# HGRN layer of a fused two-block kernel: order of the score products by width, order of VectorE's products, waits of the output product

## The chip, the cores and the metric

The kernel runs on one core of one Trainium2 chip. The metric is the device time of one execution in microseconds. Before the change the median of three executions is 1775.12 us (1773.36 to 1782.58). All data are f32.

## The reference, cut to what matters

Two transformer blocks are computed for one sequence of 512 tokens of width 1024. The first has chunked attention, a short convolution and a mixture of 32 experts. The second has two layers: an even one (mLSTM and sparse attention) and an odd one, HGRN2. The change touches the odd layer only:

```python
def hgrn2_layer(h, w_in, b_in, lb, head_norm, w_out):
    proj = h @ w_in + b_in
    fp, iv, qp, z = jnp.split(proj, 4, axis=-1)
    logf = jnp.log(lb + (1.0 - lb) * jax.nn.sigmoid(fp))
    k = (1.0 - lb) * jax.nn.sigmoid(-fp)
    q = jax.nn.silu(qp)
    o = hgrn2_chunkwise(heads(q), heads(k), heads(iv), heads(logf))
    o = rms_norm_2(o.transpose(0, 2, 1, 3), head_norm)
    return (o * jax.nn.silu(z)) @ w_out

def step(Sst, xs):                     # one chunk of one head
    bcum = jnp.cumsum(gj, axis=-2)
    dec = exp(bcum[j] - bcum[s])       # s <= j, else 0
    A = einsum('jc,sc,jsc->js', qj, kj, dec)
    o = A @ vj + (qj * exp(bcum)) @ Sst
    S_new = exp(bL)[:, None] * Sst + (kj * exp(bL - bcum)).T @ vj
```

There are 8 heads of 128 channels. The kernel takes chunks of 128 tokens, which gives the same result: four chunks a for 512 tokens.

## The kernel before, in words

**The layer's stages.** The heads go in four pairs p = 0 to 3, each with two heads c = 0, 1. For a pair TensorE computes in the order of `group(p, n)`: n = 0, 1 the forget projection of the two heads, n = 2, 3 the query projection (`feat`, 16 MATMULs of 512 columns each, two for each of 8 f32 products), then the values and the gate z. For p = 0 the latter are plain products (`tok`); for p = 1 to 3 they are one product in Winograd's form with seven sub-products (`seventh`, n = 4 to 10 of `group`, each 16 MATMULs of 256 columns). The seven share three PSUM banks a, b, c in the order a, b, a, b, c, b, c, so VectorE takes a bank after each sub-product (`seventh` of the vector program, its n = 0 to 6), and the fourth sub-product, b again, waits until the second has been taken. "Second take" is that one; "round" is one pass of p = 1 to 3.

**The scores.** A head's 128 x 128 matrix A of a chunk is cut at every 32 tokens, since exp(bcum[j] - bcum[s]) can't be factored over long distances. For query block J (32 tokens, J = 0 to 3) there is one diagonal product of keys `Km` and queries `Qm` (32 weight columns, 32 moving columns, output partitions 32J to 32J + 31) and, for J > 0, one product of all earlier keys, `KJ` (32 J weight columns: 32, 64 or 96), with queries `Qs` (output partitions 0 to 32J - 1). `step(p, "scores", c)` does first three transposes of D (the state's keys), which wait for the semaphore "pr", and then these 28 products for the four chunks a, all into one bank. `step(p, "states", c)` and `step(p, "outs", c)` are the state updates and the outputs. `PLAN` (lines 111, 112) writes down where in a round each step comes: states, outs and scores of the round before at n = 0, 1, 2, 3, 5, the scores of the pair's own first head at n = 9; `PLAN_LAST` does so for the last pair, between the parts of the output product. A step of scores thus comes eight times.

**Operands of the scores.** `prep(p, c, part)` in the vector program makes them: part 0 the cumulated logs, part 1 six differences (`Qs`, `Qm`, three blocks of `KJ`, D); ScalarE's `powers` then raises them, in the order Qs, Km, Qm, KJ, D, b and eL, each with an increment of "eE"; part 2 multiplies the powers by q or k (Qs, Qm, Km, three blocks of KJ of 128, 256 and 384 elements) and part 3 multiplies D by k and b by q, and tells "pr". `queries(p, c)` multiplies the query projection by its sigmoid. VectorE runs its program strictly in the written order: in a round `seventh` n = 0, part 2 of `prep`, `seventh` n = 1, `seventh` n = 2, part 3 and so on.

**The output product.** After the last round TensorE transposes the normed outputs y (`turn_y`; ("yT", 0, i) the heads 0 to 3 of token tile i, ("yT", 1, 0) and ("yT", 1, 2) the heads 4, 5 of two tiles each), VectorE and ScalarE copy them to `yT`, and `part(i, h, ks)` multiplies tile i by half h of the output weight. Before the first part TensorE waits for all six copies (`evacuated`).

**Lines.** L411 is every product of TensorE, L414 every transpose; L1168 is every two-operand operation of VectorE, L1179 its three-operand form, L1195 its copies, L2296 every operation of ScalarE.

Of the kernel before, what the change touches and what calls it, by code (L numbers as in the profile page):

```python
# [163 lines left out]
def build(nc, T, out):  # L164
    with ExitStack() as ctx:
# [228 lines left out]
        def tensor(pe):  # L394
# [11 lines left out]
            def evacuated(*names):  # L406
                for n in names:
                    pe.wait_ge(F[n].free, F[n].at)
# [628 lines left out]
            def stage_e():  # L1037
                def group(p, n):
                    if n < 4:
                        used[f"o_x{p}"] = feat(("fx", p, n), weight(f"o_x{p}"), n * 128)  # L1040
                    elif p:
                        for s in range(2):
                            seventh(f"o_y{p}", 2 * n - 8 + s)
                    else:
                        turned("E", n - 4)
                        used["o_y0"] = tok(("ty", n - 4), weight("o_y0"), n - 4)
                        if n in (4, 6):
                            turn("E", n // 2)

                def step(p, what, c):  # L1050
                    q, vz = pQ[p % 2][:, c, :], pvz[p % 2]
                    if what == "scores":
                        f = fill(("bt", p, c))
                        pe.wait_ge(S("pr"), saw("pr"))
                        for a in range(3):
                            ins = tr(f.ap[:, a * 128:a * 128 + 128], D[:, a * 128:a * 128 + 128])
                        ins.then_inc(f.full, 1)
                        f = fill(("ba", p, c))
                        for a in range(4):
                            for J in range(4):  # L1060
                                cj = a * 128 + 32 * J
                                if J:
                                    oo, wd, _ = KJP[J - 1]
                                    mm(f.ap[0:wd, cj:cj + 32], KJ[:, oo + a * wd:oo + a * wd + wd], Qs[:, cj:cj + 32])
                                ins = mm(f.ap[32 * J:32 * J + 32, cj:cj + 32], Km[:, cj:cj + 32], Qm[:, cj:cj + 32])
                        ins.then_inc(f.full, 1)
                    elif what == "states":
                        f = fill(("bu", p, c))
                        evacuated(("bt", p, c), *([(f"o_y{p}", "a"), (f"o_y{p}", "b")] if p else [("ty", 3)]))
                        for a in range(3):  # L1070
                            ins = mm(f.ap[:, a * 128:a * 128 + 128], KlT[:, a * 128:a * 128 + 128],
                                     vz[:, a, c * 128:c * 128 + 128])
                        ins.then_inc(f.full, 1)
                    elif what == "outs":
                        f = fill(("bo", p, c))
                        evacuated(("ba", p, c), ("bu", p, c))
                        for a in range(4):
                            o_ = f.ap[:, a * 128:a * 128 + 128]
                            ins = mm(o_, at[:, a * 128:a * 128 + 128], vz[:, a, c * 128:c * 128 + 128], True, a == 0)
                            if a:  # L1080
                                ins = mm(o_, q[:, a * 128:a * 128 + 128], St[:, a * 128 - 128:a * 128], False, True)
                        ins.then_inc(f.full, 1)

                def turn_y(name, i, ks):
                    f = fill(name)
                    for j, k in enumerate(ks):
                        ins = tr(f.ap[:, j * 128:j * 128 + 128], y4[:, i, k * 128:k * 128 + 128])
                    ins.then_inc(f.full, 1)

                def part(i, h, ks):  # L1090
                    f = fill(("oo", ks[0], i, h))
                    for k in ks:
                        ins = mm(f.ap, yT[:, k, i * 128:i * 128 + 128], ws[h][:, k * 512:k * 512 + 512], k == ks[0], k == ks[-1])
                    ins.then_inc(f.full, 1)
                for n in (4, 5, 6, 7, 0, 1, 2, 3):
                    group(0, n)
                step(0, "scores", 0)
                for p in range(1, 4):
                    for n in range(11):
                        if (p, n) == (1, 5):  # L1100
                            pe.wait_ge(S("suma"), 7)
                        group(p, n)
                        if n in PLAN:
                            what, back, c = PLAN[n]
                            step(p - back, what, c)
                        if (p, n) == (3, 9):
                            pe.wait_ge(S("yk"), 3)
                            for i in range(4):
                                turn_y(("yT", 0, i), i, range(4))
                for i in (0, 2):  # L1110
                    f = fill(("yT", 1, i))
                    for j in range(4):
                        k = 4 + j % 2
                        ins = tr(f.ap[:, j * 128:j * 128 + 128], y4[:, i + j // 2, k * 128:k * 128 + 128])
                    ins.then_inc(f.full, 1)
                ws = [weight(f"o_o{h}") for h in range(2)]
                for i in range(4):
                    evacuated(("yT", 0, i))
                for i in (0, 2):
                    evacuated(("yT", 1, i))  # L1120
                for n in range(8):
                    part(n // 2, n % 2, range(6))
                    if n in PLAN_LAST:
                        step(3, *PLAN_LAST[n])
                pe.wait_ge(S("yk"), 4)
                for i in range(4):
                    turn_y(("yT", 2, i), i, range(6, 8))
                for i in range(4):
                    evacuated(("yT", 2, i))
                    for h in range(2):  # L1130
                        part(i, h, range(6, 8))
# [8 lines left out]
        def vector(v):  # L1140
# [940 lines left out]
            def stage_e():  # L2081
# [19 lines left out]
                def prep(p, c, part):  # L2101
# [19 lines left out]
                    elif part == 1:  # L2121
                        if heads_[0]:
                            full("ba", *heads_[0])
                        heads_[0] = (p, c)
                        tt(j16(Qs), b16, bc16(bs), SUB)
                        tt(j16(Qm), b16, bc16(bm), SUB, "k1")
                        for J, (_, wd, dst) in zip((1, 2, 3), KJP):
                            tt(dst, bs4[:, :, J:J + 1].to_broadcast([128, 4, wd]), b4[:, :, 0:wd], SUB, "k2" if J == 3 else "v")
                        tt(bb.rearrange("p (a n) -> p a n", a=4), eL.unsqueeze(2).to_broadcast([128, 4, 128]), b4, SUB, "k3")
                    elif part == 2:  # L2130
                        heard("eE")
                        tt(Qs, Qs, q, MUL)
                        heard("eE", 2)
                        tt(Qm, Qm, q, MUL)
                        tt(Km, Km, kk, MUL)
                        heard("eE")
                        k4 = kk.rearrange("p (a n) -> p a n", a=4)
                        for _, wd, dst in KJP:
                            tt(dst, dst, k4[:, :, 0:wd], MUL)
                    else:  # L2140
                        heard("eE")
                        tt(bb, bb, kk, MUL)
                        heard("eE", 2)
                        tt(q, b, q, MUL, "pr")

                def scores(p, c):
                    f = full("ba", p, c)
# [53 lines left out]
                z_gain(0)  # L2201
                prep(0, 0, 0)
                prep(0, 0, 1)
                queries(0, 0)
                prep(0, 0, 2)
                prep(0, 0, 3)
                queries(0, 1)
                scores(0, 0)
                prep(0, 1, 0)
                for p in range(1, 4):  # L2210
                    y, r = f"o_y{p}", row("b_ivz" + "+" * p)
                    prep(p - 1, 1, 1)
                    states(p - 1, 0)
                    prep(p - 1, 1, 2)
                    prep(p - 1, 1, 3)
                    sums_of_weight(y)
                    queries(p, 0)
                    scores(p - 1, 1)
# [3 lines left out]
                    states(p - 1, 1)  # L2222
                    for n in range(7):
                        seventh(y, n, behind(pvz[p % 2]), by_row(r))
                        if n == 0:
                            prep(p, 0, 2)
                        elif n == 2:
                            row_done(r)
                            prep(p, 0, 3)
                        elif n == 3:  # L2230
                            pair_squares(p - 1)
                        elif n == 4:
# [14 lines left out]
                    h_add(i, h, full("oo", k0, i, h))  # L2247
                prep(3, 1, 1)
                states(3, 0)
                prep(3, 1, 2)  # L2250
                prep(3, 1, 3)
                for n in range(3):
                    part(n // 2, n % 2, 0)
                scores(3, 1)
# [846 lines left out]
```

## Time and profile before

| | |
|---|---|
| runs | 1773.36, 1775.12, 1782.58 us |
| profiled execution | 1776.3 us, span 1774.5 us |
| mean granted TensorE clock | 0.985 |
| TensorE (PE) busy | 1711.0 us, 96% |
| weight loads (PEld) busy | 1000.1 us, 56% |
| VectorE (DVE) busy | 864.8 us, 49% |
| ScalarE (ACT) busy | 372.5 us, 21% |
| GpSimd (POOL) busy | 209.7 us, 12% |
| DMA | 308.61 MB, queue q1 40.1% and q0 2.9% of 16 engines |

The profile is of one execution; its own time is 1776.3 us, and the span from the first to the last instruction 1774.5. Times in rows are microseconds from the span's start. Busy times of PE are modelled ends of pipelined matmuls: two rows that follow without a gap overlap by part of the last MATMUL. The granted clock is a share of 2.4 GHz and has two levels in this trace, 1.0 and 0.5. The HGRN layer runs from about 1450 us to the end.

### The profile page before, as it was taken

Reading aid. Unit: us, or ns where it says so; the run is one execution under the profiler, and the core shown is the slowest. Engines: PE = TensorE matmul, PEld = TensorE weight load, DVE = VectorE, ACT = ScalarE, POOL = GpSimd, SP = SyncE. Lnnn points to the kernel's source line nnn. Section 1 sums busy time; section 2 is a strip of 40 time slices with the busy share of each in tenths; the row PEclk is TensorE's granted clock in tenths of the full one; section 3 lists DMA queues with packets and bytes.
Section 4 is the critical chain, followed back from the end, with each engine's and each line's share of the span. In section 5 each row is a group of like instructions: output and inputs, shape, how many; then the busy total and the mean of one; then the engine's idle time right before and its main releaser. Section 6 shows DMA issues by size and latency. Waiting matters only on the chain.

```text
span 1774.5 us, 19612 instructions
## 1 busy us (share of the span) xinstructions
PE 1711.0 (96%) x7538; PEld 1000.1 (56%) x7538; DVE 864.8 (49%) x1505; ACT 372.5 (21%) x659; POOL 209.7 (12%) x280
## 2 busy tenths in 40 slices
PE   7999999998899999999999999999799999999999
PEld 3878877675433333333434464768655544767664
DVE  3756743445332323232325348666755555557653
ACT  1122220001100000100003113320244325344430
POOL 1234310001000000000001100011145300000000
PEclk9999999998999999999999999999999999999999
DMA  7322121255699999999991214032300021112101
GB/s 279 113 88 91 48 107 53 95 221 206 270 403 426 427 425 428 426 427 424 427 397 60 71 48 125 42 120 101 128 22 1 13 92 63 48 48 95 48 1 48
DMA packets 27873, 308.61 MB, mean 174 GB/s; under 512 B 4415, under 2 KB 4703, under 8 KB 10368
## 3 DMA queue, kind: packets, MB, share of 16 engines
q1 hardware_dynamic: 21312, 289.21, 40.1%
q0 software_dynamic: 6464, 18.10, 2.9%
q8 instruction: 62, 1.02, 0.2%
q14 instruction: 35, 0.29, 0.0%
HBM read 306.57 MB, written 4.19 MB: 175 GB/s over the span
## 4 chain that ended last, share of the span: by engine, by line
PE 88%; DVE 7%; ACT 1%; DMA 1%; issue 1%; POOL 0%; DVEq 0%; SPq 0%; ACTq 0%
PE ps L411 84%; PE ps L414 5%; DVE arena L1168 4%; ACT arena L2296 1%; DVE arena L1179 1%; DMA arena<-in_rows 1%; DVE wring L1168 0%; DVE arena L1195 0%; DMA wring<-in_dense 0%; DVE small L1183 0%; DVE arena L1264 0%; POOL small L2708 0%; ACT L2296 0%; DVE HT L1195 0%; DVE H L1168 0%
## 5 line engine op out<-in xcount | busy, mean ns | idle before, releaser
L411 PE MATMUL ps<-arena 128*64 128x512 f32 (+13 forms) x2384 | 532.9, 400 | 10.5 <-DVE arena L1173 3.8
L411 PE MATMUL ps<-wring,arena 128*64 128x512 f32 (+2 forms) x1136 | 397.7, 580 | 5.0 <-DVE H L1168 2.5
L411 PEld LDWEIGHTS ps<-arena 128*64 128x64 f32 (+3 forms) x2384 | 244.0, 154 | 232.9 <-issue 216.9
L411 PE MATMUL ps<-wring,HT 128*128 128x512 f32 (+1 forms) x1040 | 362.9, 502 | 5.1 <-ACT HT L2296 1.9
L1168 DVE TENSOR_TENSOR arena<-ps,arena 128x512 f32<-128x512 f32 (+1 forms) x197 | 134.9, 685 | 466.1 <-PE ps L411 307.1
L411 PEld LDWEIGHTS ps<-wring,HT 128*128 128x128 f32 x1040 | 194.3, 191 | 143.6 <-issue 127.6
L2296 ACT ACTIVATE arena<-ps 128x512 f32<-128x512 f32 (+3 forms) x163 | 88.4, 543 | 629.9 <-PE ps L414 325.5
L411 PEld LDWEIGHTS ps<-wring,arena 128*64 128x64 f32 (+1 forms) x1136 | 148.5, 155 | 125.6 <-issue 122.1
L411 PE MATMUL ps<-HT,wring 128*128 128x512 f32 (+2 forms) x528 | 196.1, 537 | 0.5 <-DVE arena L1195 0.5
L411 PE MATMUL ps<-wring 128*128 128x256 f32 x816 | 189.3, 387 | 5.1 <-DVE arena L1168 5.1
L1168 DVE TENSOR_TENSOR H<-ps,H 128x512 f32<-128x512 f32 x182 | 125.9, 692 | 103.5 <-PE ps L411 93.1
L411 PEld LDWEIGHTS ps<-wring 128*128 128x128 f32 x816 | 155.7, 194 | 30.3 <-DVE arena L1168 7.1
L2296 ACT ACTIVATE arena<-arena 128x512 f32<-128x512 f32 (+10 forms) x123 | 85.2, 692 | 355.3 <-DVE arena L1168 335.5
L411 PEld LDWEIGHTS ps<-HT,wring 128*128 128x128 f32 (+1 forms) x528 | 98.1, 191 | 88.2 <-issue 82.5
L1168 DVE TENSOR_TENSOR arena<-arena 128x512 f32<-128x512 f32 (+12 forms) x203 | 123.3, 607 | 19.6 <-ACT arena L2296 7.2
L414 PEld LDWEIGHTS ps<-con,arena 128*128 128x128 f32 (+4 forms) x762 | 92.9, 159 | 62.7 <-issue 50.6
L414 PE MATMUL ps<-con,arena 128*128 128x128 f32 (+4 forms) x762 | 107.9, 283 | 19.6 <-DVE arena L1179 10.8
L1195 DVE COPY arena<-ps 128x512 f32<-128x512 f32 (+7 forms) x126 | 70.3, 558 | 91.6 <-PE ps L411 66.2
L411 PE MATMUL ps<-HT,arena 128*64 128x512 f32 (+1 forms) x272 | 106.0, 542 | 4.1 <-issue 3.4
L2296 ACT ACTIVATE arena<-arena,small 128x128 f32<-128x128 f32 (+3 forms) x124 | 66.5, 536 | 124.2 <-DVE small L1264 113.6
L411 PEld LDWEIGHTS ps<-HT,arena 128*64 128x64 f32 (+1 forms) x272 | 41.4, 155 | 61.0 <-issue 57.7
L1264 DVE CUSTOM_DVE_ANT_0 arena<-ps,arena 128x512 f32<-128x512 f32 (+3 forms) x96 | 47.2, 492 | 45.0 <-PE ps L411 34.7
(106 smaller groups left out, 951.9 us busy)
## 6 DMA issues: line engine op xcount, KB each, us to landing
wring<-in_w SPq DMA_DIRECT2D x48, 2048.0 KB, 20.2
wring<-in_dense SPq DMA_DIRECT2D x39, 2048.0 KB, 8.1
arena<-in_w SPq DMA_DIRECT2D x36, 2048.0 KB, 17.8
HT<-in_w SPq DMA_DIRECT2D x12, 2048.0 KB, 16.8
arena<-in_rows POOLq DMA_DIRECT2D x33, 256.0 KB, 5.1
H<-in_x SPq DMA_DIRECT2D x4, 512.0 KB, 4.2
arena<-in_relb POOLq DMA_DIRECT2D x8, 256.0 KB, 8.2
n_scratch<-arena POOLq DMA_DIRECT2D x4, 512.0 KB, 3.2
```

Of the source, the lines that this page charges most:

```text
L411: return nc.tensor.matmul(o, l, r, start=start, stop=stop, skip_group_check=True)
L414: return nc.tensor.transpose(o, i, ident[0:i.shape[0], 0:i.shape[0]])
L1168: done(nc.vector.tensor_tensor(o, a, b, op), tell)
L1179: done(nc.vector.scalar_tensor_tensor(o, a, s, b, op0, op1), tell)
L1195: done(nc.vector.tensor_copy(o, i), tell)
L1264: done(nc.vector.tensor_tensor_reduce(o, a, b, -1.0, 3.0e38, ADD, MIN, low), tell)
L2296: ins = nc.scalar.activation(o, i, fn, **k)
```

## The change

It has three parts. In `step(p, "scores", c)` all 16 diagonal products come first and then the others by J, so that weights of 32, 64 and 96 columns follow each other in three groups. The output product waits only for the copies of its own tile. VectorE's parts 2 and 3 of `prep` are cut into queries, keys, blocks, state and out; in a round, queries and keys come after `seventh` n = 0, the three products of the blocks after n = 1, state and out after n = 2, and the first wait is for three exponentials at once. For the very first head, keys, blocks and state come before `queries(0, 0)`. The number of operations of each engine and the DMAs are unchanged.

```diff
--- before.py
+++ after.py
@@ -1059,10 +1059,11 @@
                         for a in range(4):
                             for J in range(4):
                                 cj = a * 128 + 32 * J
-                                if J:
-                                    oo, wd, _ = KJP[J - 1]
-                                    mm(f.ap[0:wd, cj:cj + 32], KJ[:, oo + a * wd:oo + a * wd + wd], Qs[:, cj:cj + 32])
-                                ins = mm(f.ap[32 * J:32 * J + 32, cj:cj + 32], Km[:, cj:cj + 32], Qm[:, cj:cj + 32])
+                                mm(f.ap[32 * J:32 * J + 32, cj:cj + 32], Km[:, cj:cj + 32], Qm[:, cj:cj + 32])
+                        for J, (oo, wd, _) in zip((1, 2, 3), KJP):
+                            for a in range(4):
+                                cj = a * 128 + 32 * J
+                                ins = mm(f.ap[0:wd, cj:cj + 32], KJ[:, oo + a * wd:oo + a * wd + wd], Qs[:, cj:cj + 32])
                         ins.then_inc(f.full, 1)
                     elif what == "states":
                         f = fill(("bu", p, c))
@@ -1114,11 +1115,9 @@
                         ins = tr(f.ap[:, j * 128:j * 128 + 128], y4[:, i + j // 2, k * 128:k * 128 + 128])
                     ins.then_inc(f.full, 1)
                 ws = [weight(f"o_o{h}") for h in range(2)]
-                for i in range(4):
-                    evacuated(("yT", 0, i))
-                for i in (0, 2):
-                    evacuated(("yT", 1, i))
                 for n in range(8):
+                    if n % 2 == 0:
+                        evacuated(("yT", 0, n // 2), ("yT", 1, n // 4 * 2))
                     part(n // 2, n % 2, range(6))
                     if n in PLAN_LAST:
                         step(3, *PLAN_LAST[n])
@@ -2127,21 +2126,34 @@
                         for J, (_, wd, dst) in zip((1, 2, 3), KJP):
                             tt(dst, bs4[:, :, J:J + 1].to_broadcast([128, 4, wd]), b4[:, :, 0:wd], SUB, "k2" if J == 3 else "v")
                         tt(bb.rearrange("p (a n) -> p a n", a=4), eL.unsqueeze(2).to_broadcast([128, 4, 128]), b4, SUB, "k3")
-                    elif part == 2:
-                        heard("eE")
+                    elif part == "queries":
                         tt(Qs, Qs, q, MUL)
-                        heard("eE", 2)
                         tt(Qm, Qm, q, MUL)
+                    elif part == "keys":
                         tt(Km, Km, kk, MUL)
+                    elif part == "blocks":
                         heard("eE")
                         k4 = kk.rearrange("p (a n) -> p a n", a=4)
                         for _, wd, dst in KJP:
                             tt(dst, dst, k4[:, :, 0:wd], MUL)
-                    else:
+                    elif part == "state":
                         heard("eE")
                         tt(bb, bb, kk, MUL)
+                    else:
                         heard("eE", 2)
                         tt(q, b, q, MUL, "pr")
+
+                def weighed(p, c, part):
+
+                    if part == 0:
+                        heard("eE", 3)
+                        prep(p, c, "queries")
+                        prep(p, c, "keys")
+                    elif part == 1:
+                        prep(p, c, "blocks")
+                    else:
+                        prep(p, c, "state")
+                        prep(p, c, "out")
 
                 def scores(p, c):
                     f = full("ba", p, c)
@@ -2201,9 +2213,12 @@
                 z_gain(0)
                 prep(0, 0, 0)
                 prep(0, 0, 1)
+                heard("eE", 3)
+                for x in ("keys", "blocks", "state"):
+                    prep(0, 0, x)
                 queries(0, 0)
-                prep(0, 0, 2)
-                prep(0, 0, 3)
+                prep(0, 0, "queries")
+                prep(0, 0, "out")
                 queries(0, 1)
                 scores(0, 0)
                 prep(0, 1, 0)
@@ -2211,8 +2226,8 @@
                     y, r = f"o_y{p}", row("b_ivz" + "+" * p)
                     prep(p - 1, 1, 1)
                     states(p - 1, 0)
-                    prep(p - 1, 1, 2)
-                    prep(p - 1, 1, 3)
+                    for x in range(3):
+                        weighed(p - 1, 1, x)
                     sums_of_weight(y)
                     queries(p, 0)
                     scores(p - 1, 1)
@@ -2222,11 +2237,10 @@
                     states(p - 1, 1)
                     for n in range(7):
                         seventh(y, n, behind(pvz[p % 2]), by_row(r))
-                        if n == 0:
-                            prep(p, 0, 2)
-                        elif n == 2:
+                        if n < 3:
+                            weighed(p, 0, n)
+                        if n == 2:
                             row_done(r)
-                            prep(p, 0, 3)
                         elif n == 3:
                             pair_squares(p - 1)
                         elif n == 4:
@@ -2247,8 +2261,8 @@
                     h_add(i, h, full("oo", k0, i, h))
                 prep(3, 1, 1)
                 states(3, 0)
-                prep(3, 1, 2)
-                prep(3, 1, 3)
+                for x in range(3):
+                    weighed(3, 1, x)
                 for n in range(3):
                     part(n // 2, n % 2, 0)
                 scores(3, 1)
```

## Rows read from the trace of the kernel before

**Rows 1.** Busy time and clock by stretch: the HGRN layer, 1440 us on.

```profile
1440.00:1775.00 335.00, 323.14 (x1431) 200.69 (x1429) 183.54 (x306) 116.20 (x153) 7.65 (x8) 0.97 0.14 51
```

**Rows 2.** Waits from 1440 us on, TensorE: us, times, longest.

```profile
PE ps L411 <- DVE arena L1168: 3.3, 3, 1.1
```

**Rows 3.** Timeline of TensorE, the last round: start us, us, idle before.

```profile
1586.91 4.01 PE L411 MATMUL ps<-arena 128*32 128x32 f32 x56
1590.86 7.13 PE L411 MATMUL ps<-HT,wring 128*128 128x512 f32 x16
...
1605.41 1.72 PE L411 MATMUL ps<-arena 128*128 128x128 f32 x14
1606.97 3.62 PE L411 MATMUL ps<-wring,HT 128*128 128x256 f32 x16
1611.69 3.72 PE L411 MATMUL ps<-wring 128*128 128x256 f32 x16 [1.10 <-DVE arena L1168]
```

**Rows 4.** Timeline of TensorE inside the scores at 1586.91, narrow windows.

```profile
1587.15 0.30 PE L411 MATMUL ps<-arena 128*64 128x32 f32 x2
...
1587.39 0.25 PE L411 MATMUL ps<-arena 128*32 128x32 f32 x2
...
1587.57 0.35 PE L411 MATMUL ps<-arena 128*96 128x32 f32 x2
...
1587.85 0.32 PE L411 MATMUL ps<-arena 128*32 128x32 f32 x8
...
1588.10 0.30 PE L411 MATMUL ps<-arena 128*64 128x32 f32 x2
```

**Rows 5.** Groups by form, 1440 us on: weight loads, mean ns.

```profile
L411 PEld LDWEIGHTS ps<-arena 128*32 128x32 f32 x320 | 12.5, 112 | 4.1 <-issue 1.3
...
L411 PEld LDWEIGHTS ps<-arena 128*96 128x96 f32 x64 | 8.4, 173 | 1.4
L411 PEld LDWEIGHTS ps<-arena 128*64 128x64 f32 x64 | 6.3, 139 | 1.4
```

**Rows 6.** Timeline of ScalarE and VectorE, the last round, around the second take.

```profile
1601.06 4.50 ACT L2296 ACTIVATE arena<-arena 128x512 f32<-128x512 f32 x7 [0.98 <-DVE arena L1168]
...
1598.75 0.75 DVE L1179 SCALAR_TENSOR_TENSOR arena<-ps,pcl,arena 128x512 f32<-128x512 f32 x1 [4.00 <-ACT arena L2296]
...
1607.17 3.66 DVE L1168 TENSOR_TENSOR arena<-arena 128x512 f32<-128x512 f32 x6
1610.94 1.49 DVE L1168 TENSOR_TENSOR arena<-ps,arena 128x512 f32<-128x512 f32 x2
```

**Rows 7.** Timeline of three engines around the first scores.

```profile
1475.44 4.51 ACT L2296 ACTIVATE arena<-arena 128x512 f32<-128x512 f32 x7
...
1482.89 5.25 DVE L1168 TENSOR_TENSOR arena<-arena 128x512 f32<-128x512 f32 x8
...
1488.29 0.52 PE L414 MATMUL ps<-con,arena 128*128 128x128 f32 x3 [1.94 <-DVE arena L1168]
1488.74 5.27 PE L411 MATMUL ps<-arena 128*32 128x32 f32 x56
1493.95 8.65 PE L411 MATMUL ps<-HT,wring 128*128 128x512 f32 x16
```

**Rows 8.** Timeline of three engines where the output product begins.

```profile
1702.17 0.60 ACT L2296 ACTIVATE arena<-ps 128x512 f32<-128x512 f32 x1 [4.43 <-PE ps L414]
...
1703.18 0.69 DVE L1195 COPY arena<-ps 128x512 f32<-128x512 f32 x1 [0.75 <-PE ps L414]
...
1704.12 5.39 PE L411 MATMUL ps<-wring,arena 128*128 128x512 f32 x12 [0.98 <-DVE arena L1195]
```

**Rows 9.** Stretches behind the scores at 1518.82 and 1554.47: busy, clock.

```profile
1523.00:1526.00 3.00, 3.00 (x8) 1.32 (x8) 2.69 (x6) 0.35 (x1) 0.00 (x0) 1.00 0.00 0
1559.00:1562.00 3.00, 3.00 (x9) 2.42 (x8) 2.65 (x7) 0.00 (x0) 0.00 (x0) 0.52 0.00 0
```

**Rows 10.** Timeline of TensorE, the product behind the scores at 1554.47.

```profile
1558.42 5.41 PE L411 MATMUL ps<-wring 128*128 128x256 f32 x16
```

## Prediction

> **What bounds the kernel now.** I read the page first, whose busy times stand in the table above: TensorE is busy for 96% of the span, so time is won only by shortening what TensorE does or by closing its gaps. The change touches the last layer alone, so the next view is the table of stretches: from 1440 us on TensorE is busy 323.1 of 335 us at a mean granted clock of 0.97, VectorE 183.5, ScalarE 116.2 [rows 1]. The list of waits shows what ends TensorE's gaps: three of 1.1 us each, ended by VectorE [rows 2]; the timeline puts one in each of the three rounds of the head pairs, in front of the fourth step of the seven-product scheme [rows 3]. Two more gaps are single: 1.94 us ahead of the first scores [rows 7] and 0.98 us ahead of the output product [rows 8]. The rest is TensorE's own work, and in it the reader is to look at one item: the scores, 28 small products (56 MATMULs, two for each f32 product) that take 4.01 us [rows 3] and occur eight times.
>
> **Edit 1, order inside the scores.** The narrow windows show where these 4 us go [rows 4]. From 1587.85 on, eight MATMULs of 32 weight columns start within 0.12 us (a row of 0.32 us, less the 0.20 us that one takes), some 17 ns apart. The next one, 64 columns wide, starts at 1588.10, 0.13 us after the last. The 64-wide pair keeps 1587.15 to 1587.39, 0.24 us; the 32-wide pair behind it 0.18; the 96-wide pair 1587.57 to 1587.85, 0.28; the eight 0.25. These 0.95 us are one of four blocks, and four make 3.8. In each block the width changes four times, and every change costs about 0.13 to 0.15 us. The new order changes it twice: 40 MATMULs of 32 columns, 8 of 64, 8 of 96.
> Cost of the new order, term by term. The 32-wide: not below 17 ns each (the start spacing of the eight) and not above 31 (0.25/8, with a change in it) [rows 4]; I take 25, since the last eight all write the same partitions, which only part of the burst does. 39 spacings and a change: 0.98 + 0.13 = 1.11 (0.81 to 1.34). The 64-wide: one load lasts 139 ns against 112 for 32 columns and 173 for 96 [rows 5], so 32 columns more cost 27 to 34 ns; a load of 64 then takes about 55 ns of its own, the lower bound; the upper is half a pair with its change, 0.24/2 = 120. I take 65, nearer to the loads, as the pairs' 120 holds the very change that is gone. Seven and a change of 0.15: 0.61 (0.54 to 0.99). The 96-wide in the same way: 80 to 140, I take 90: 0.63 and 0.11 for the way out, 0.74 (0.64 to 1.16). Sum 2.45 us, between 2.0 and 3.5. Eight times 3.95 - 2.45 (the next product starts 3.95 after the first small one [rows 3]) is **12.0 us** (3.6 to 15.6). Nothing else hides it: TensorE is the path before and behind. VectorE waits 4.00 us for ScalarE's sigmoid of the fourth projection, which follows TensorE's row, before 1598.75 [rows 6]; both move up with TensorE.
>
> **Edit 2, the blocks' keys behind the second take.** In each round VectorE does six products with the powers, 3.66 us from 1607.17, and only then, at 1610.94, the take that the fourth step's bank waits for [rows 6]. TensorE would be free at 1610.42 (1606.97 + 3.62, less the 0.17 by which back-to-back rows overlap, as 1605.41 + 1.72 against 1606.97) and starts at 1611.69; its first row then takes 3.72 and not 3.62 [rows 3]. So 1.27 + 0.10 is lost. The change moves three of the six (128, 256 and 384 elements) behind the take. The eight of the first round take 5.25 us [rows 7]; they are the same six and two large ones, so a large one costs 0.8 with its wait, three large ones 2.4, and the three small ones about 1.3 us. The take ends near 1610.3, before TensorE needs it. Gain 3 x 1.37 = **4.1 us**. The margin is only 0.1 us, but a shortfall costs only itself. The new wait for three exponentials at once costs nothing in the rounds: they are the first three of the seven that ScalarE begins at 1601.06, done by 1603.1, 4 us before VectorE comes to them [rows 6]. What is late next is the third take and the product that frees the next transposes; both are queued behind the moved work for 1.3 us and TensorE comes to the transposes only some 8 us later.
>
> **Edit 3, the first round.** VectorE stands idle before 1482.89 while ScalarE has begun the seven exponentials at 1475.44 and ended them at 1479.95 [rows 7]. The change puts keys, blocks and state there (five of the eight products, 2.9 us) and leaves three behind the sigmoid: 3 x 0.8 = 2.4 us, so the transposes may start at about 1485.3. TensorE is free at 1486.36 and today starts at 1488.29 [rows 7]. The gap of 1.94 goes, with the overlap **2.1 us**.
>
> **Edit 4, the output product.** It waits for all six evacuations; the last is VectorE's copy from 1703.18 to 1703.87, which only the third tile needs, while ScalarE's for the first tile starts at 1702.17 and takes 0.60 [rows 8]. TensorE's transposes end 0.98 before 1704.12. Gap, overlap and the slower first row: **1.2 us**. The added waits of tiles 2 to 4 fall 5 us apart on copies that are done.
>
> **The clock.** Behind five of the eight score stretches the granted clock falls: it is 1.00 behind the scores at 1518.82 and 0.52 behind those at 1554.47 [rows 9], that is 2.4 and 1.2 GHz. The product that follows there takes 5.41 us, not 3.62 [rows 3, 10], 1.8 us lost; three more stretches of this kind cost 1.65 to 1.8 each by the same comparison. The first is longer: scores 5.27 for 4.01, projection 8.65 for 7.13 [rows 3, 7], 2.8 us. Together **9.8 us**. What TensorE did before each fall is 4 us of narrow products, in the first case with a gap of 1.94 us ahead. Nothing else in the layer does this, and three such stretches passed without a fall. With 2.45 us in place of 4, I expect nearly all falls to go. The Trainium skill ties the lower clock to an idle TensorE ("TensorE: Matmul & The Clock Gate", HAM oscillation). The trace does not agree: these falls follow a busy engine. By that rule packing a busy stretch would bring nothing back; that is the second case below.
>
> **Sum.** 12.0 + 4.1 + 2.1 + 1.2 = 19.4 us, with the clock 29.2. The profiled execution took 1776.3 us (span 1774.5 and 1.8 around it); the median of three, 1775.1, lies 1.2 below. 1775.1 - 29.2 = 1745.9; I say **1746 us**.
>
> **The rivals.**
> A. As above, 1746; with the scores at 2.0 us 1742, at 3.5 us 1754. For it: four widths' changes per block stand in the rows. Chance 0.69.
> B. The clock falls as often as before: 19.4 us gained, 1756; with the dear end of the scores 1764. For it: five falls of eight is no rare event and the stretches stay narrow. Against: three did not fall at 4 us. Chance 0.20.
> C. The order of widths makes no difference, because each small product waits for its own load. Then 56 loads and products cost the same in any order, the clock falls as before, and only edits 2 to 4 count: 1775.1 - 7.4 = 1768. Against it: loads of 112 ns [rows 5] whose MATMULs start 17 ns apart [rows 4] do overlap. The skill states such a rule (same page, What overlaps and what doesn't: a load overlaps a running MATMUL only where the rows of the array differ), and all 56 use all 128 rows; by that rule this case is right, and the trace speaks against it. Chance 0.05.
> D. Slower. The blocks' products now follow one another into the same partitions from 0 on, where before a diagonal one stood between. If each of them then waited for the one before it as it now waits at a change, a pair would cost 0.18, 0.24 or 0.28 us by width [rows 4]; if the diagonal ones did too, 20 x 0.18 + 4 x 0.24 + 4 x 0.28 = 5.7 us, 1.7 more than today, eight times 13.8; longer narrow stretches would let the clock fall in the three spared places as well, 5.4 more; less 7.4 is 11.8: 1787. It decides for slower once a score stretch exceeds about 5 us. Against: the eight in [rows 4] hold two products in a row of one region and do not wait. Chance 0.02.
> E. A wait takes the place of the three gaps: the take is late by more than the margin, or VectorE, with 30 us less around its 184 [rows 1], holds the transposes. At most the 4.1 us return: 1750. Chance 0.04.
>
> **How the numbers follow.** About 9 us is what a measurement of this kernel can tell from no change (0.5%). A, B and E lie beyond it: 0.93. C lies within: 0.05. Slower is D: 0.02. The range takes A with its bounds and most of B: 1740 (A's cheap end, and the spread of the runs) to 1760.
>
> **What would show it.** Each score row should take about 2.5 us and show the forms in order, with two waits of about 0.13 us. Above 3.5, A is wrong. The three waits of 1.1 on VectorE should be gone from the list, or be under 0.3; the idle ahead of 1488.29 and 1704.12 likewise. The granted clock from 1440 us on should be 1.00 or 0.99, not 0.97; if it stays, B holds. A new TensorE wait on VectorE or ScalarE of over 1 us would be E. The other layers should not move.

## The result and the profile after

| | before | after |
|---|---|---|
| median | 1774.61 us (1773.36 to 1782.58, 4 runs) | 1745.65 us (1743.40 to 1746.51, 4 runs) |
| profiled execution | 1776.3 us, span 1774.5 | 1746.37 us, span 1744.4 |
| mean granted clock | 0.985 | 0.990 |

The ratio is 0.9817, 95% interval 0.9802 to 0.9833: 29.0 us faster, where 1746 us and 29.2 were forecast. (A fourth run, 1774.10 us, stands beside the three that gave 1775.12 before.) The page of the changed kernel (busy time, share, instructions) and its row of granted clock in 40 slices:

```profile
PE 1685.1 (97%) x7538; PEld 982.5 (56%) x7538; DVE 864.5 (50%) x1505; ACT 372.6 (21%) x659; POOL 210.3 (12%) x280
...
PEclk9999999999899999999999999999989999999999
```

TensorE has 26 us less work with the same 7538 MATMULs, and the other engines are as they were. The stretch from 1440 us on, in the columns of [rows 1]:

```profile
1440.00:1745.00 305.00, 299.04 (x1438) 184.24 (x1436) 183.85 (x307) 116.35 (x154) 7.67 (x8) 1.00 0.15 57
```

The clock is 1.00 where it was 0.97, and TensorE is busy for 299 of 305 us. The layer itself is best measured from its first projection, which begins behind the same wait of 1.04 us in both. Timeline of TensorE, before:

```profile
1451.75 7.13 PE L411 MATMUL ps<-wring,HT 128*128 128x512 f32 x16 [1.04 <-ACT HT L2296]
```

and after:

```profile
1454.74 7.13 PE L411 MATMUL ps<-wring,HT 128*128 128x512 f32 x16 [1.04 <-ACT HT L2310]
```

From there to the end are 322.75 us before (to 1774.5) and 289.7 after (to 1744.4): the layer gained **33.1 us**. The span gained only 30.1, since in this execution the layer began 3.0 us later, in code that the change does not touch. In the thirteen traces of this study the layer begins anywhere between 1451.8 and 1455.3 us, the changed kernel's second one at 1454.4.

The last round on TensorE, the rows that answer to [rows 3]:

```profile
1575.76 2.07 PE L411 MATMUL ps<-arena 128*32 128x32 f32 x56
1577.67 7.11 PE L411 MATMUL ps<-HT,wring 128*128 128x512 f32 x16
...
1593.76 3.62 PE L411 MATMUL ps<-wring,HT 128*128 128x256 f32 x16
1597.21 3.62 PE L411 MATMUL ps<-wring 128*128 128x256 f32 x16
```

The score stretch keeps TensorE from 1575.76 to 1577.67, 1.91 us where it was 3.95, and the same in all eight steps. The fourth step of the seven starts at 1597.21, right at the end of the row before it (1593.76 + 3.62, less the overlap), with no idle time. VectorE in that round, against [rows 6]:

```profile
1593.96 2.14 DVE L1167 TENSOR_TENSOR arena<-arena 128x512 f32<-128x512 f32 x3
1596.20 0.69 DVE L1167 TENSOR_TENSOR arena<-ps,arena 128x512 f32<-128x512 f32 x1
1597.00 1.34 DVE L1167 TENSOR_TENSOR arena<-arena 128x128 f32<-128x128 f32 x3
```

The three products of queries and keys end at 1596.1, the second take at 1596.89, 0.3 us before TensorE needs it, and the three small products now come behind it, 1.34 us. The first scores and the output product, against [rows 7, 8]:

```profile
1489.18 0.49 PE L414 MATMUL ps<-con,arena 128*128 128x128 f32 x3
...
1677.25 0.66 PE L414 MATMUL ps<-con,arena 128*128 128x128 f32 x4 [0.59 <-DVE arena L1167]
1677.74 5.32 PE L411 MATMUL ps<-wring,arena 128*128 128x512 f32 x12
```

The first transposes start without a wait, and the output product starts right behind the last transposes. Those wait for 0.59 us in place of 0.35. The list of waits has only this of TensorE's in the layer, beside the one at the layer's start:

```profile
PE ps L411 <- ACT HT L2310: 1.0, 1, 1.0
...
PE ps L414 <- DVE arena L1167: 0.6, 1, 0.6
```

Inside the scores (narrow windows, against [rows 4]):

```profile
1575.76 0.45 PE L411 MATMUL ps<-arena 128*32 128x32 f32 x30
...
1575.76 0.69 PE L411 MATMUL ps<-arena 128*32 128x32 f32 x40
...
1576.39 0.65 PE L411 MATMUL ps<-arena 128*64 128x32 f32 x8
...
1576.97 0.86 PE L411 MATMUL ps<-arena 128*96 128x32 f32 x8
```

The first row is a part of the second: 30 MATMULs of 0.20 us each that all start within 0.25 us. The forty of 32 columns keep 1575.76 to the start of the 64-wide ones at 1576.39; eight of 64 to 1576.97, eight of 96 to 1577.67. The weight loads of the forty (rows of PEld):

```profile
1575.76 0.58 PEld L411 LDWEIGHTS ps<-arena 128*32 128x32 f32 x40 [0.17 <-issue]
```

Each load lasts 106 to 113 ns, which would be over 4 us one behind another, and all forty lie within 0.58 us: many of them run at the same time.

### The profile page after: what moved, and what is told of

Its sections match the earlier page's. It is cut to its first block, busy times and chain, and to the rows that moved or that the text cites. A ratio compares the mean times of both kernels' runs of the same rounds, so it can differ in the third digit from the quotient of the medians.

```text
span 1744.4 us, 19605 instructions
## 1 busy us (share of the span) xinstructions
PE 1685.1 (97%) x7538; PEld 982.5 (56%) x7538; DVE 864.5 (50%) x1505; ACT 372.6 (21%) x659; POOL 210.3 (12%) x280
## 4 chain that ended last, share of the span: by engine, by line
PE 89%; DVE 5%; DMA 3%; issue 1%; ACT 1%; POOL 0%; SPq 0%; DVEq 0%; ACTq 0%
PE ps L411 85%; PE ps L414 4%; DVE arena L1167 2%; DMA wring<-in_w 2%; DMA arena<-in_rows 1%; DVE arena L1178 1%; ACT arena L2310 1%; DVE arena L1194 1%; DMA wring<-in_dense 0%; DVE small L1182 0%; DVE arena L1263 0%; POOL small L2722 0%; DVE wring L1167 0%; DVE HT L1194 0%; DVE H L1167 0%
## 5 line engine op out<-in xcount | busy, mean ns | idle before, releaser
L411 PE MATMUL ps<-arena 128*64 128x512 f32 (+13 forms) x2384 | 516.3, 398 | 11.1 <-DVE arena L1172 3.8
L411 PEld LDWEIGHTS ps<-arena 128*64 128x64 f32 (+4 forms) x2384 | 232.3, 154 | 228.9 <-issue 217.7
L411 PE MATMUL ps<-wring 128*128 128x256 f32 x816 | 185.2, 381 | 1.8 <-DVE arena L1167 1.8
```

What stands on the lines that cost most here:

```text
L411: return nc.tensor.matmul(o, l, r, start=start, stop=stop, skip_group_check=True)
```

## The experiments

**The new order alone.** On the kernel before:

```diff
-                                if J:
-                                    ...
-                                ins = mm(f.ap[32 * J:32 * J + 32, cj:cj + 32], ...)
+                                mm(f.ap[32 * J:32 * J + 32, cj:cj + 32], ...)
+                        for J, (oo, wd, _) in zip((1, 2, 3), KJP):
+                            for a in range(4):
+                                cj = a * 128 + 32 * J
+                                ins = mm(f.ap[0:wd, cj:cj + 32], ...)
```

> The kernel before with the new order of the score products and nothing else. Theory (width changes cost about 0.13 us each, and a long narrow stretch lets the clock fall): each of the eight score stretches keeps TensorE 1.90 us (3.95 before), the clock stays at 1.00 from 1440 us on or falls once at most, the three waits of 1.1 us, the 1.94 and the 0.98 us stay: 1774.6 - 16.3 - 8 to 10, so 1748 to 1752 us. Rival (the clock falls because TensorE waits for VectorE): the falls stay, 1758 us.

Measured: 1755.19 us, ratio 0.9862 (0.9845 to 0.9878). The layer takes 298.8 us. Timeline of TensorE around the first scores and around a second take:

```profile
1491.88 0.52 PE L414 MATMUL ps<-con,arena 128*128 128x128 f32 x3 [1.94 <-DVE arena L1169]
1492.33 2.55 PE L411 MATMUL ps<-arena 128*32 128x32 f32 x56
1494.69 8.32 PE L411 MATMUL ps<-HT,wring 128*128 128x512 f32 x16
...
1604.24 3.72 PE L411 MATMUL ps<-wring 128*128 128x256 f32 x16 [1.10 <-DVE arena L1169]
...
1615.12 2.07 PE L411 MATMUL ps<-arena 128*32 128x32 f32 x56
```

The waits of 1.94 and 1.10 us are there as before, the score stretches are 1.90 us but for the first. The granted clock falls once, for 3.4 us from inside the first scores on, where the wait of 1.94 precedes them; that costs about 1.7 us (2.36 us there for 1.90, and a projection of 8.32 us for 7.11). The time is 3 us above the forecast's upper end. The forecast started from the kernel before at 1774.6 us, and beside this run that kernel took 1778.90: the gain in the whole time is 23.7 us, within the 22.6 to 26.6 that the forecast comes to. In the layer the order alone gives 23.9 us: 16.3 of shorter stretches, and 7.6 left over, which is put down to the clock.

**Everything but the new order.** The changed kernel with the old loop over a and J:

> The changed kernel with the old order of the score products; VectorE's order and the waits of the output product stay changed. Theory: score stretches of 3.95 us again, the waits of TensorE on VectorE gone, the clock falls behind several of the eight score stretches (3 to 8): 1745.7 + 16.3 + 5 to 10, so 1765 to 1772 us, ratio to before 0.996. Rival (the falls come from the waits): no falls, 1760 to 1762 us.

Measured: 1766.21 us, ratio 0.9929 (0.9913 to 0.9946); the layer takes 310.8 us. Timeline of TensorE, first scores and those of a round:

```profile
1488.89 4.28 PE L411 MATMUL ps<-arena 128*32 128x32 f32 x56
...
1552.02 4.01 PE L411 MATMUL ps<-arena 128*32 128x32 f32 x56
1555.96 3.72 PE L411 MATMUL ps<-wring 128*128 128x256 f32 x16
```

The stretches are 3.95 us again and the waits on VectorE stay away. But the clock falls at two of the eight only, and begins to fall inside them (the first, 3.4 us, with no wait ahead of it, and the last, 6.8), not at five: the product at 1555.96 runs at full speed where before it took 5.41 [rows 10]. So the falls of before were not the old order's alone; closing the waits, or the place where the stretches then came to lie, took three of five away; no run separates these two. The time lies in the range that I gave, with fewer falls than I gave; the ratio of 0.996 that I gave lies above the measured interval.

**What lets the clock fall: length or pauses.** The changed kernel, all 28 products computed twice, which gives the same values again:

```diff
+                        for again in range(2):
+                            ...
```

> The changed kernel with all 28 score products computed twice into the same places, in the new order: narrow stretches of 3.8 us with few width changes. Theory (the clock falls because the stretch of narrow products is long): falls come back behind several of the eight, 1745.7 + 15.2 + 4 to 10, 1765 to 1771 us. Rival (the falls belong to the pauses at the width changes): none, 1761 us.

Measured: 1762.65 us, ratio 0.9900 (0.9884 to 0.9917). Timeline of one stretch, and then the stretch from 1440 us on, where the third number from the end is the clock:

```profile
1581.34 4.07 PE L411 MATMUL ps<-arena 128*32 128x32 f32 x112
```

```profile
1440.00:1760.00 320.00, 314.62 (x1885) 199.03 (x1883) 183.55 (x306) 116.20 (x153) 7.65 (x8) 1.00 0.14 53
```

The stretch is 3.9 us of narrow products, as long as before the change, and there is no fall behind any of the eight. My theory of the prediction, that about 4 us of narrow products are enough for a fall, does not hold. The counterpart is the old order twice:

> The changed kernel with all 28 score products computed twice, in the old order: stretches of 7.8 us with sixteen pauses each and more. Theory after e5 (the clock falls where the array stands in pauses at width changes, not because the products are narrow): falls behind or inside all eight stretches, each of 3.4 us or more. Rival (the falls of before were chance or came from the waits on VectorE): two or fewer of the eight.

Measured: 1816.02 us (one run). One stretch, then the clock (third from the end) in two parts of that stretch and behind three of the eight:

```profile
1600.46 8.66 PE L411 MATMUL ps<-arena 128*32 128x32 f32 x112
```

```profile
1603.50:1606.40 2.90, 2.90 (x50) 2.38 (x43) 0.00 (x0) 1.42 (x2) 0.00 (x0) 1.00 0.00 0
1606.50:1609.00 2.50, 2.50 (x22) 2.03 (x21) 0.00 (x0) 0.00 (x0) 0.00 (x0) 0.50 0.02 7
```

```profile
1496.80:1499.80 3.00, 3.00 (x6) 1.44 (x5) 2.22 (x6) 0.00 (x0) 0.00 (x0) 0.50 0.01 3
...
1571.70:1574.70 3.00, 3.00 (x8) 2.47 (x8) 2.62 (x6) 0.00 (x0) 0.00 (x0) 0.50 0.00 0
...
1687.50:1690.50 3.00, 3.00 (x6) 1.45 (x5) 2.59 (x6) 0.00 (x0) 0.00 (x0) 0.50 0.00 0
```

In all eight stretches the clock falls to 0.50 inside the stretch and stays there behind its end, 6.8 us or 10.2 in all. The same 112 MATMULs with few pauses (3.9 us) left it at 1.00. So at 3.9 us narrow products in close order kept the clock, and with the pauses at the width changes they lost it at five or two of eight (3.95 us) and at all eight (8.6 us). Whether the pauses as such or the smaller amount of work in the same time is what counts, these runs can't separate. A close stretch of more than 3.9 us was not run either, so length may still play a part beside the pauses, and each of these counts comes from one trace.

**Where the time inside a stretch goes.** Diagonal products by output partitions (32 of them, from 32J on, are called a region below):

```diff
-                        for a in range(4):
-                            for J in range(4):
+                        for J in range(4):
+                            for a in range(4):
```

> The changed kernel with the 16 diagonal products in the order of their output partitions (eight MATMULs in a row into the same 32 partitions) in place of chunk by chunk. Theory (MATMULs of 32 columns keep 31 ns in the same partitions, 8 ns on average in changing ones): a score stretch takes 1.90 - 0.26 + 32 x 0.031 = 2.6 us. Rival (only the width counts, partitions don't): 1.90 us.

Measured: 1748.25 us (one run), the layer 292.6. The stretch, and its first 40 MATMULs alone:

```profile
1575.80 2.43 PE L411 MATMUL ps<-arena 128*32 128x32 f32 x56
```

```profile
1575.80 1.05 PE L411 MATMUL ps<-arena 128*32 128x32 f32 x40
```

From 1575.80 to the next row's start are 2.26 us, between the two forecasts. So partitions do count, but half as much as I gave: the 40 MATMULs of 32 columns start within 0.85 us (1.05 less the 0.20 of one), where the change has them within 0.49 (0.69 less 0.20). That is 22 ns each and not the 31 of the same region throughout. Where eight of one region meet the eight of the next, the start times in the trace show single ones 5 to 6 ns behind another, so a few run beside each other.

Widths of 64 and 96 alternating:

```diff
-                        for J, (oo, wd, _) in zip((1, 2, 3), KJP):
-                            for a in range(4):
+                        for J, a in [(1, a) for a in range(4)] + [(J, a) for a in range(4) for J in (2, 3)]:
```

> The changed kernel with the products of 64 and of 96 columns alternating, chunk by chunk, in place of four and four: seven changes between 64 and 96 for one. Theory (every change of width costs about 0.1 us more than going on in the same width): 1.90 + 6 x 0.095 = 2.5 us a stretch. Rival (only changes from and to 32 columns cost): 1.90 us.

Measured: 1748.98 us (one run), the layer 295.2. One stretch:

```profile
1575.03 2.76 PE L411 MATMUL ps<-arena 128*32 128x32 f32 x56
```

The next row starts at 1577.62: 2.59 us for 1.91. Six more changes cost 0.69 us, 0.115 each. Every change of width costs, not only those from and to 32 columns. The clock falls at none of the eight stretches here, nor in the run before.

**No change of width at all.** Since MATMULs into different regions start beside each other, the wide products can be cut into regions. In the loop over a and J, in place of the order of the change:

```diff
+                                for i in range(J):
+                                    ks = KJP[J - 1][0] + a * 32 * J + 32 * i
+                                    mm(f.ap[32 * i:32 * i + 32, cj:cj + 32], KJ[:, ks:ks + 32], Qs[:, cj:cj + 32])
+                                ins = mm(f.ap[32 * J:32 * J + 32, cj:cj + 32], Km[:, cj:cj + 32], Qm[:, cj:cj + 32])
```

> The changed kernel with every product of 64 or 96 weight columns cut into products of 32, each into its own 32 partitions: no width change inside the scores, but 80 MATMULs for 56. Theory (a width change costs 0.12 us, MATMULs of 32 columns into changing regions 8 ns, into the same region 31 ns): the first region gets 32 of the 80, 1.0 us, and a stretch takes 1.15 to 1.4 us in place of 1.90; eight times 0.5 to 0.75, 1740 to 1742 us. Rival (small MATMULs are bound by their number, 24 ns each and more): 1.9 us and more, no gain, 1746 us or slower.

```profile
1603.33 0.49 PE L414 MATMUL ps<-con,arena 128*128 128x128 f32 x3
1603.75 1.20 PE L411 MATMUL ps<-arena 128*32 128x32 f32 x80
```

Eighty MATMULs take 1.13 us (1603.75 to 1604.88) where 56 took 1.91, and the layer 283.6 us. The first region's 32 at 31 ns give 1.0, and all eighty start within 1.00 us (1.20 less the 0.20 of one). The sum fits; that this region is the bound is concluded from it. The time is 1739.84, ratio 0.9781 (0.9764 to 0.9797), 5.8 us less than the change took. To see both on one chip:

> The changed kernel as it is, as the measure for the next one on the same chip: ratio to before 0.982 to 0.984.

> The kernel with all score products of 32 columns again, beside the changed kernel on the same chip. Theory: score stretches of 1.13 us against 1.90, eight times, 6.2 us faster than the changed kernel, ratio to before 0.979. Rival (the gain seen was the spread between runs): less than 3 us between the two.

```profile
1573.68 1.20 PE L411 MATMUL ps<-arena 128*32 128x32 f32 x80
```

Measured: the changed kernel 1745.58 us (1743.60 to 1746.19, ratio 0.9805, 0.9790 to 0.9821), the all-32 kernel 1741.36 (1739.37 to 1742.18, ratio 0.9783, 0.9767 to 0.9799). The changed kernel's ratio lies below the 0.982 to 0.984 that I gave for it: beside these runs the kernel before took 1778.40 us. The runs of the two do not overlap, the medians differ by 4.2 us, between the rival's 3 and the forecast's 6.2; the layers in the traces by 289.7 - 283.6 = 6.1, eight times 0.78 less rounding, as forecast. The intervals against the kernel before overlap a little, so the size of the gain in the whole time is known less well than its sign.

**VectorE's order in the rounds.** The three products of the blocks back ahead of the second take:

```diff
                         prep(p, c, "keys")
+                        prep(p, c, "blocks")
                     elif part == 1:
-                        prep(p, c, "blocks")
+                        pass
```

> The changed kernel with the three products of the blocks' keys back ahead of the second take in each round. Theory: the three waits of TensorE on VectorE of about 1.1 us come back, 3 x 1.37 = 4.1 us in the layer, nothing else moves. Rival (once the scores are shorter VectorE has slack there): no waits, no loss.

Measured: 1747.27 us (one run). From the list of waits:

```profile
PE ps L411 <- DVE arena L1167: 3.1, 3, 1.0
```

Three waits are back and the layer takes 293.6 us, 3.9 more. The clock does not fall.

**The first head and the output product.**

```diff
-                heard("eE", 3)
-                for x in ("keys", "blocks", "state"):
-                    prep(0, 0, x)
                 queries(0, 0)
-                prep(0, 0, "queries")
-                prep(0, 0, "out")
+                heard("eE", 3)
+                for x in ("queries", "keys", "blocks", "state", "out"):
+                    prep(0, 0, x)
```

and the output product waits for all six copies again, as before the change.

> The changed kernel with edits 3 and 4 taken back: the first head's products all behind the sigmoid, and the output product waits for all six copies. Theory: the wait of 1.9 us ahead of the first scores and the one of 1.0 us ahead of the output product come back, 3.3 us in the layer. Rival (the change only moves these waits): TensorE's idle time in the layer doesn't change by more than 1 us. As to the clock: if a wait beside a dense narrow stretch is enough for a fall, as in the run with the new order alone, one fall of 3.4 us comes at the first scores.

Measured: 1751.79 us (one run). Timeline of TensorE at both places:

```profile
1490.08 0.52 PE L414 MATMUL ps<-con,arena 128*128 128x128 f32 x3 [1.86 <-DVE arena L1169]
1490.52 2.69 PE L411 MATMUL ps<-arena 128*32 128x32 f32 x56
1493.03 9.43 PE L411 MATMUL ps<-HT,wring 128*128 128x512 f32 x15
...
1683.15 2.38 PE L411 MATMUL ps<-wring,arena 128*128 128x512 f32 x5 [0.98 <-DVE arena L1196]
```

Both waits are back, with 3.3 us. The layer takes 296.3, 6.6 more than with the change: the other 3.3 are the clock, which falls inside the first scores, for 6.8 us (2.51 us for 1.91, and 9.43 for fifteen MATMULs behind them). I had given one fall of 3.4. Edit 3 is thus worth more than its wait: with a wait of 1.9 us ahead of a narrow stretch the clock fell even where the stretch has few pauses. It did so in both kernels that had the wait with the new order, each in one trace, and in none of the others with the new order did a fall come at the scores.

## Why the prediction was right, and where it was not

**The sum against the layer's 33.1 us.** Scores 8 x (3.95 - 1.91) = 16.3, where 12.0 was forecast. Blocks' keys 3.9, forecast 4.1. First head and output product 3.3, forecast 2.1 + 1.2. These are 23.5; the rest, 9.6, is put down to the clock, forecast 9.8. It can be had directly too: from score stretch to the next transposes, less the 2.04 us that the stretch itself is shorter, the five falls cost 2.8, 1.7, 1.7, 1.7 and 1.6 us beside the changed kernel, 9.4 in all. Case A held in the time, with its scores beyond the cheap end (1.91 us, where 2.0 was the least), and the waits went that were said to go.

**The term that was mis-sized is the 32-wide part of edit 1.** I gave it 1.11 us with its change, and not below 0.81; it takes 0.63 (1575.76 to 1576.39). The 64-wide part takes 0.58 (forecast 0.61) and the 96-wide 0.70 (0.74). The burst of eight in [rows 4] was taken as the fastest rate, 17 ns. By the order of the kernel it was mixed: two of its MATMULs go into the last region, four into the first and two into the second, so its 17 ns is an average over both cases, the same region and another. The new order goes round the four regions: the first 30 start within 0.25 us, some 8 ns apart. Only the last eight, all into the first region, stand 31 to 32 ns apart by their start times, which I gave to none and averaged into 25. I had the reason (same partitions) and applied it to the average only.

**Why the time was met all the same.** The scores gave 4.3 us more, and the part ahead of the layer took 3.0 us more in the profiled execution. The forecast of 1746 owes its closeness to that offset, which is luck; the layer alone was forecast 29.2 and gave 33.1. Beside the last runs, where the kernel before took 1778.40 us, the changed kernel gained 32.8.

**The clock: right in amount, not in cause.** The forecast "with 2.45 us in place of 4, I expect nearly all falls to go" came true, and its reason, the length of the stretch, did not hold: a dense stretch of 3.9 us has none. The runs point to the density, together with the waits: the order alone left one fall of five, the other edits alone two. The two sums (7.6 us of clock by the order, 4.7 by the rest) can't be added, since together they would be more than the 9.6 that was there: both take away some of the same falls. Whether a stretch of 1.9 us with as many pauses as before would have kept the clock was not run. The Trainium skill ("TensorE: Matmul & The Clock Gate", HAM oscillation) ties the lower clock to an idle engine; its example is a wait of about 3 to 5 us for a DMA. The traces agree in part: the two falls with the new order came behind an idle time of 1.9 us, shorter than that. But eight of eight fell in the run with the old order twice, where TensorE's waits on other engines in the layer come to 0.3 us beside the one at its start.

**The rivals.** B (clock as before) is out: 1.00 in the layer. C (order makes no difference since each load waits) is out: forty loads of 106 to 113 ns lie within 0.58 us, although all use 128 rows, and 80 MATMULs take 1.13 us. The rule of the Trainium skill that was named for it ("TensorE: Matmul & The Clock Gate", What overlaps and what doesn't) does not hold here. D (same region waits fully) is out: 31 ns, not 180. E did occur in a small way: the last transposes wait 0.59 us for VectorE in place of 0.35. The margin of the second take is 0.3 us, not the 0.1 forecast: the three large products take 2.14 us and not 2.4.

## What to carry to other kernels

Where small f32 products of different widths stand in one sequence, look at the start times inside the row: the merged row says "busy", yet half of it was pauses. Sort them by width, or better, cut them all to 32 columns and go round the output regions; more MATMULs can be faster. A stretch of small products with pauses can cost a second time, through the granted clock of what follows, and here so could a wait ahead of it; both are worth closing.

## What the runs showed that was not expected

- 80 f32 MATMULs of 32 x 32 columns run in 1.13 us, 14 ns each with the way out, against 34 ns each for 56 in three widths and 70 ns for 56 with sixteen changes.
- In one region a MATMUL takes 31 ns at 32 columns; those of 64 and of 96 columns take about 60 and 87 on average (the rows of eight above, less one MATMUL of 0.22 and 0.25 us, by seven), and 58 and 85 behind the first two by their start times. A change of width costs 0.115 us above that.
- The granted clock fell to 0.50 at eight of eight stretches of 8.6 us with many changes of width, at five or two of eight of 3.95 us, and at none of eight of 3.9 us with few changes.
